# ConvFFN up projection as seven half-width products per tile pair, with the gated activations and the residual spilled to DRAM

## What is computed

```python
def dwconv(x, w, b):            # three taps along the tokens, per channel
    ...
def conv_ffn(hn, w_up, conv_w, conv_b, w_down):
    u = dwconv(hn @ w_up, conv_w, conv_b)
    gate, val = jnp.split(u, 2, axis=-1)
    return (jax.nn.silu(gate) * val) @ w_down
```

## Time and profile before

| | |
|---|---|
| median of three runs | 2789.49 us (2786.89 to 2789.79) |
| the profiled execution, whole | 2791.05 us |
| its span, first to last instruction | 2789.4 us |
| TensorE busy | 97% of the span |
| VectorE, ScalarE, GpSimd busy | 44%, 27%, 7% |
| mean granted TensorE clock | 0.989 |
| DMA | 369 MB, 132 GB/s over the span |

### The profile page before, as it was taken

How to read it: one execution, slowest core, us unless ns; L and a number is a source line. 1 busy time by engine, 2 the same in 40 slices (tenths; PEclk the granted TensorE clock), 3 DMA queues, 4 the chain that set the end, 5 groups by cost and what they waited for, 6 DMA issues and landing times.

```text
span 2789.4 us, 31604 instructions
## 1 busy us (share of the span) xinstructions
PE 2692.7 (97%) x12356; PEld 2087.6 (75%) x12356; DVE 1213.7 (44%) x1282; ACT 746.6 (27%) x840; POOL 194.9 (7%) x197
## 2 busy tenths in 40 slices
PE   4999999999899897999999999999999999999997
PEld 3788888887444444788888888888888888888886
DVE  5534433672543367336533433444334343244345
ACT  3222111222233224223322212232122221132222
POOL 1000000000134145000000000000000000000000
PEclk9999999999999999999999999999999999999999
DMA  9765555783170521422222223222232222322222
GB/s 353 299 236 210 203 204 203 293 307 142 51 151 12 149 77 66 168 90 99 83 95 101 78 93 116 90 90 83 97 106 90 102 84 93 112 90 94 88 93 102
DMA packets 99777, 369.13 MB, mean 132 GB/s; under 512 B 21744, under 2 KB 39200, under 8 KB 69208
## 3 DMA queue, kind: packets, MB, share of 16 engines
q1 hardware_dynamic: 74832, 278.26, 29.3%
q0 software_dynamic: 10880, 72.55, 6.9%
q10 hardware_dynamic: 14000, 17.44, 1.7%
HBM read 346.48 MB, written 21.74 MB: 132 GB/s over the span
## 4 chain that ended last, share of the span: by engine, by line
PE 57%; DVE 1%; DMA 0%; ACT 0%; issue 0%; DVEq 0%; ACTq 0%
PE f_ps L2157 56%; PE f_first_ps L2194 0%; DVE h L2124 0%; PE f_ps L2168 0%; PE f_late_ps L2168 0%; DVE x_lo L2052 0%; DMA h<-in_xT 0%; DVE f_lo L1964 0%; DVE f_square_sum L2004 0%; DMA f_raw<-in_w_out 0%; ACT f_hi L1832 0%; DVE f_full L2046 0%; DVE h L1994 0%; DVE f_square_sum L2000 0%; DVE h L1982 0%
## 5 line engine op out<-in xcount | busy, mean ns | idle before, releaser
L2157 PE MATMUL f_ps<-x_hi,f_hi 128*128 128x512 f32 x1600 | 627.2, 392 | 4.3 <-DVE f_lo L1964 2.5
L2157 PE MATMUL f_ps<-x_hi,f_lo 128*128 128x512 f32 x1600 | 629.6, 393 | 0.0
L2157 PE MATMUL f_ps<-x_lo,f_hi 128*128 128x512 f32 x1600 | 628.2, 393 | 0.0
L1964 DVE TENSOR_TENSOR f_lo<-f_raw,f_hi 128x2048 fp32r<-128x2048 f32 (+1 forms) x164 | 333.3, 2032 | 109.2 <-ACT f_hi L1832 97.0
L1832 ACT ACTIVATE f_hi<-f_raw 128x2048 fp32r<-128x2048 f32 (+1 forms) x164 | 278.6, 1699 | 291.4 <-PE f_ps L2157 285.6
L2157 PEld LDWEIGHTS f_ps<-x_hi,f_hi 128*128 128x128 f32 x1600 | 300.9, 188 | 73.3 <-DVE f_lo L1964 3.3
L2157 PEld LDWEIGHTS f_ps<-x_lo,f_hi 128*128 128x128 f32 x1600 | 300.9, 188 | 69.3
L2157 PEld LDWEIGHTS f_ps<-x_hi,f_lo 128*128 128x128 f32 x1600 | 300.7, 188 | 66.8
L2157 PE MATMUL f_ps<-f_u_hi,f_hi 128*128 128x512 f32 x682 | 267.9, 393 | 0.0
L2157 PE MATMUL f_ps<-f_u_lo,f_hi 128*128 128x512 f32 x682 | 267.4, 392 | 0.0
L2157 PE MATMUL f_ps<-f_u_hi,f_lo 128*128 128x512 f32 x682 | 267.0, 392 | 0.0
(11 more groups left out here) (309 smaller groups left out, 3113.3 us busy)
## 6 DMA issues: line engine op xcount, KB each, us to landing
f_raw<-in_w_up SPq DMA_DIRECT2D x86, 1024.0 KB, 4.8
i_ring<-in_ada_rest POOLq DMA_DIRECT2D x64, 1024.0 KB, 5.3
f_raw<-in_w_down SPq DMA_DIRECT2D x64, 704.0 KB, 4.1
i_raw<-in_w_in SPq DMA_DIRECT2D x38, 1024.0 KB, 4.8
i_ring<-in_ada_first SPq DMA_DIRECT2D x32, 1024.0 KB, 7.4
f_raw<-in_w_out SPq DMA_DIRECT2D x16, 1024.0 KB, 4.8
g_ring<-rrow SPq DMA_DIRECT2D x24, 256.0 KB, 3.6
i_raw<-in_w_first POOLq DMA_DIRECT2D x16, 320.0 KB, 5.1
```

The source lines that it names most:

```text
L1964: nc.vector.tensor_tensor(w_lo[s][:, 0:kt, :], raw[s][:, 0:kt, :], w_hi[s][:, 0:kt, :].bitcast(F32), ALU.subtract).then_inc(lo_ok, 1)
L2157: mm = nc.tensor.matmul(pt[s][:, :], w[s][:, k, :], v[:, c, :], start=(k == 0 and n == 0), stop=(k == len(slots) - 1 and n == 2))
```

## The change

In the up projection, two tile pairs (`PLAIN = 2`) are computed as before. Each of the 42 others (`PAIRS`) is computed as a 2 by 2 block product, with one level of Strassen's scheme in Winograd's form. The blocks of the weights are: gate tile with k steps 0 to 7 (a11) and 8 to 15 (a12), value tile likewise (a21, a22). The blocks of the input are k steps 0 to 7 and 8 to 15, each for the early and the late 256 tokens. Instead of eight block products there are seven (q = 0 to 6), each of 8 k steps and three passes: 24 matmuls of 128x256.

- Weights: GpSimd makes four sums of blocks per pair, each 128x1024 (`block_sums`). ScalarE and VectorE split the seven left operands into high and low parts (`block_high`, `block_low`, 128x1024 each) in four half-tile slots.
- Input: GpSimd makes four sums of input blocks once, in place in the memory of `h`, as 32 operations of 128x256; ScalarE and VectorE split them (`form_high`, `form_low`).
- Outputs: some products accumulate on top of each other in PSUM. ScalarE copies four of the partial results into an SBUF tile `f_c` (`part_copy`), VectorE adds three (`part_add`). The taps then read `f_c` instead of PSUM (`block_middle`, `block_outer`).
- Memory: the gated product's parts are written to DRAM by SyncE (`put_u`, 44 tiles of 512 KB) and read back by GpSimd's queue ahead of each group's down tiles. The residual `h` is written to DRAM tile by tile by GpSimd's queue, since its memory is used for the sums, and read back before the first down tile ends.
- Order: all up tiles come first, then the 64 down tiles, group by group. `normed` writes in place into `h`. The first pair's weights lose their own staging: they go through `raw[0]` and `raw[1]`, whose loads wait until the output projection's last tiles are split.

```diff
-        first_raw = [ground.at("f_first_raw0", [P, KT, P], 0), ground.at("f_first_raw1", [P, KT, P], 106112)]
...
+        bank = [[pt[0], pt[1], pb[0]], [pb[1], pf[0], pf[1]]]
+        SLOT = (0, 1, 2, 3, 0, 1, 2)
+        FIRST_ORDER, ORDER = (0, 1, 2, 3, 4, 5, 6), (3, 0, 1, 2, 4, 5, 6)
...
+            @block.gpsimd
+                for m in range(KT):
+                    pool.wait_ge(ev_ok, m + 1)
+                    pool.dma_start(hd[:, m, :], h[:, m, :]).then_inc(h_st[max(0, m - KT + 3)], 16)
...
+                for k in range(HK):
+                    pool.wait_ge(hl, KT + k + 1)
+                    nc.gpsimd.tensor_tensor(h[:, k, LATE], h[:, k, LATE], h[:, k, EARLY], ALU.subtract).then_inc(ts_ok, 1)
+                for k in range(HK):
+                    pool.wait_ge(hl, KT + HK + k + 1)
+                    pool.wait_ge(ts_ok, HK)
+                    nc.gpsimd.tensor_tensor(h[:, HK + k, LATE], h[:, HK + k, LATE], h[:, k, LATE], ALU.subtract).then_inc(ts_ok, 1)
...
+                def block_sums(i, par, r):
+                    a11, a12, a21, a22 = (block_of(par, n) for n in range(4))
+                    s0, s1, s2 = (b[:, :, :] for b in S_buf)
+                    pool.wait_ge(sl[par], 32 * (r + 1))
+                    if positive(i):
+                        pool.wait_ge(bl_ok, split_by(i - 1, 5))
+                    nc.gpsimd.tensor_tensor(s0, a21, a22, ALU.add).then_inc(bs_ok, 1)
+                    pool.wait_ge(bs_ok, 4 * i + 1)
+                    nc.gpsimd.tensor_tensor(s1, s0, a11, ALU.subtract).then_inc(bs_ok, 1)
+                    nc.gpsimd.tensor_tensor(s2, a11, a21, ALU.subtract).then_inc(bs_ok, 1)
+                    pool.wait_ge(bs_ok, 4 * i + 2)
+                    pool.wait_ge(bl_ok, split_by(i, 1))
+                    nc.gpsimd.tensor_tensor(s0, a12, s1, ALU.subtract).then_inc(bs_ok, 1)
...
+            def block_high(act, i, q, par, r):
+                if q in (0, 3, 6):
+                    act.wait_ge(sl[par], 32 * (r + 1))
+                else:
+                    act.wait_ge(bs_ok, 4 * i + (1, 2, None, 3, 4)[q - 1])
+                if q >= 4:
+                    act.wait_ge(pq_ok, 7 * i + q - 3)
+                elif positive(i):
+                    act.wait_ge(pq_ok, 7 * (i - 1) + (5, 6, 7, 4)[q])
...
+                nc.scalar.activation(slot_of(w_hi, q), source(par, q), ACT.Copy).then_inc(bh_ok, 1)
...
-                    act.wait_ge(first_ld[s], 16)
-                    nc.scalar.activation(first_hi[s][:, :, :], first_raw[s][:, :, :], ACT.Copy).then_inc(hi_ok, 1)
+                    act.wait_ge(w_ld[s], 16 * (KT // 2 + 1))
+                    nc.scalar.activation(first_hi[s][:, :, :], raw[s][:, :, :], ACT.Copy).then_inc(hi_ok, 1)
...
+                    if n == KT + HK:
+                        act.wait_ge(w_ld[1], 16 * (KT // 2 + 2))
+                        nc.scalar.activation(w_hi[1][:, :, :], raw[1][:, :, :], ACT.Copy).then_inc(hi_ok, 1)
...
+            def block_low(dve, i, q, par):
+                dve.wait_ge(bh_ok, split_by(i, q))
+                nc.vector.tensor_tensor(slot_of(w_lo, q), source(par, q), slot_of(w_hi, q).bitcast(F32), ALU.subtract).then_inc(bl_ok, 1)
...
+                def opening(i, par):
+                    block_low(dve, i, 4, par)
+                    u_low(dve, i - 1 + PLAIN, 1 - par)
+                    block_low(dve, i, 5, par)
+                    block_low(dve, i, 6, par)
...
+                def closing(i, par):
+                    last = isinstance(i, int) and i == PAIRS - 1
+                    part_add(dve, i, 3, par)
...
+                        block_low(dve, i + 1, 3, 1 - par)
+                    part_add(dve, i, 4, par)
...
+                        block_low(dve, i + 1, 0, 1 - par)
+                    part_add(dve, i, 5, par)
...
+                        block_low(dve, i + 1, 1, 1 - par)
...
+                    block_outer(dve, i, 0)
+                    block_outer(dve, i, 1)
...
+                        block_low(dve, i + 1, 2, 1 - par)
+                    times(dve, i + PLAIN, (cv_ok, 2 * i + 2))
...
+            def part(pe, i, q, par):
+                pe.wait_ge(bl_ok, split_by(i, q))
...
+                for k in range(HK):
+                    high, low = form(q, k)
+                    for n, (w, v) in enumerate(((a, high), (a, low), (b, high))):
+                        mm = nc.tensor.matmul(to[:, 0:HALF_T], w[:, k, :], v, start=(q in (0, 1, 3) and k == 0 and n == 0),
+                                              stop=(k == HK - 1 and n == 2), skip_group_check=True)
+                mm.then_inc(pq_ok, 1)
```

More of the change, by code:

```diff
@@ L1692, in stage_tail @@
 def stage_tail(nc, A, out, ground, ps, sem, ones, eps, mod, sc_ffn, gfcol, early):
-    UP = 2 * GT
-    PER = UP + KT
-    SLOTS = GT + 1
-    with ExitStack() as ctx:
[L1698 to L1708, removed]
-        x_hi, x_lo, x_raw = early["x_hi"], early["x_lo"], early["x_raw"]
+    PLAIN = 2
@@ new lines, in _ @@
+                for i in range(2):
+                    turn(i, i)
+                with sp.Fori(1, PAIRS // 2 - 1) as r:
+                    for s in range(2):
+                        turn(2 * r + s, s)
+                last = PAIRS - 1
+                sp.wait_ge(bl_ok, split_by(last - 1, 6))
+                for s in range(2):
+                    load_down(0, s, s)
+                put_u(last - 1 + PLAIN, 0)
+                for n in range(3):
+                    sp.wait_ge(h_st[n], 16 if n else 16 * (KT - 2))
@@ new lines, in _, with get_u, kept @@
+                turns(pool, block_sums)
+                def get_u(g, a, b, signal):
+                    for j in range(a, b):
+                        pool.dma_start(u_in[g % 2][j][:, :, :], ud[GT * g + j, :, :, :]).then_inc(signal, 16)
+                def kept(tiles):
+                    for n in range(2):
+                        pool.wait_ge(u_st[n], 32 * ((tiles + 1 - n) // 2))
+                last = PAIRS - 1
+                kept(GT)
+                pool.wait_ge(pq_ok, 7 * last + 2)
@@ L1922, in place @@
[L1922 to L1931 removed]
+                middle(act, 0, 0)
@@ L2093, in ups @@
-                def ups(g):
-                    with dve.Fori(1, GT - 1) as j:
-                        pair(g, j, KT)
-                    pair(g, GT - 1, KT if g + 1 < GROUPS else GT)
-                pair(0, 0, KT)
-                ups(0)
+                split_lo_into(dve, F0 + 4, w_lo[1], raw[1], w_hi[1])
+                times(dve, 0, (ev_ok, F0 + 2))
+                for k in range(HK):
+                    form_low(dve, 1, k)
+                u_low(dve, 0, 0)
+                for k in range(HK):
+                    form_low(dve, 2, k)
@@ L2099, in _, with turn @@
+                def turn(i, par, r):
+                    if not (isinstance(i, int) and i == 0):
+                        opening(i, par)
+                    closing(i, par)
+                turns(dve, turn)
+                split_lo(dve, D0 + 1, 1, GT)
+                u_low(dve, FT - 1, 1)
                 for g in range(GROUPS):
                     final = g == GROUPS - 1
-                    if not final:
-                        pair(g + 1, 0, GT)
-                    t = down_tile(g, 0)
@@ L2228, in _ @@
[L2228 to L2235 removed]
+                    product(pe, F0 + 2 + s, s, every, in_hi, in_lo, free=(read_ok, 1 + s))
```

559 lines of the change are left out of this document (402 added, 157 removed).

## The result

The changed kernel takes 2823.68 us (median of four runs, 2820.87 to 2826.23), beside 2788.19 for the kernel before (four runs, 2785.55 to 2789.79): a ratio of 1.0126, with a 95% interval of 1.0114 to 1.0138. It is slower by 35 us; the forecast was slower by 11. The profiled run took 2826.23 us, 35.2 above the profiled run of before, with a span of 2824.6.

A forecast was written before the change was run, and what follows sets the result against it. TensorE bounds the old kernel; the new bound is mutually exclusive VectorE and GpSimd SBUF work, 22.0 us per pair. Terms sum to +11 on 2791.05: 2802 profiled, 2800 us median; range 2760 to 2840 (80%).

The forecast's parts named there:

- 40 pairs in the middle, -4: Up projection loop: 22.0 us per pair instead of 22.1, -4 us, bounds -56 to +32.
- First and last pair, -4.2: Both ends of the up loop: these two pairs run at TensorE's pace, 2 x -2.1 us.
- First pair's weights, +3.5: Opening: without own staging their second load waits for the output projection's last low part, +3.5 us (2 to 6).
- Input sums +10, ScalarE +1: Late half's normalizing: 32 input-block sums hold VectorE back, +10 us (4 to 15); ScalarE's extra high part, +1 (0 to 2).
- Pair 0 in addition, +3.7: First block pair: leftover VectorE form work and GpSimd's first block sums make product 2 wait, +3.7 us (0 to 8).
- "the loads are a pair ahead. 0.": DMA: spilling 23 MB out and in costs 0, since the DMA is busy a quarter of the time and loads run ahead.
- Hand-over to the down tiles, +1: Up to down tiles: three 512 KB reads issued one product ahead, 8.4 us for 1.5 MB, +1 us (0 to 3).
- Down tiles, 0: Down projection: 33 matmuls per tile, the same work at the same 0.230 us, so no change.
- TensorE stays the bound: Rival for the up loop: the exclusion does not hold or the work fits into gaps; -80 us, 2709 us; 10%.
- Losses covered: Rival for the up loop: exclusion holds but its losses are covered, 21.2 to 21.7 us per pair, 2768 to 2788; 20%.
- GpSimd keeps the turn between its second and third sum: Rival for the up loop: VectorE's low part comes 2.2 us later, 22.6 to 22.9 us per pair, 2824 to 2836; 18%.
- The clock falls: Rival for the up loop: TensorE's clock drops in the new gaps, 2.4 us per pair, about 2895 us; 5%.

The follow-up runs named there:

- the PSUM run: Changed kernel with the assembled conv input in two idle PSUM banks, so the four taps read PSUM again, nothing left out: 2745.21 us, ratio 0.9848 to the kernel before.
- the run without the sums: Changed kernel with the 32 sums of input blocks at the opening cut to 16 of their 256 columns: 2812.43 us (one run).
- small sums: Changed kernel with each of GpSimd's four block sums cut to 16 of 1024 elements from the second block pair on: 2742.38 us (one run).
- fills: Changed kernel with each block sum, from the second block pair on, replaced by a 16-element sum and two fills reading nothing from SBUF: 2740.74 us (one run).

## Why the prediction was right, and where it was wrong

The mechanism in the loop and the sign were right, but the size was not: +35 us for +11, with the missing 24 at the start and the end of the loop. The largest decision, that the exclusion and not TensorE sets the loop's pace, came out to the number: 22.05 us per pair for 22.0. The rows of 4.51 and 1.21 us bore it, and the two operations in 0.89 us bore the exemption that the PSUM run then used.

- *40 pairs in the middle, -4*: -2.2. The 22.0 was a sum of 22.4 with savings and losses of 1.65 and 1.3, and held to 0.05; the savings and losses were not measured one by one, so that some of this closeness may be luck. TensorE's wait came where it was put, ahead of product 2, 1.9 us at most.
- *First and last pair, -4.2*: the last one as said; the first is buried in the step to pair 1.
- *First pair's weights, +3.5*: 3.2.
- *Input sums +10, ScalarE +1*: 9.2 together, and 9.0 by the run without the sums, at the same clock.
- *Pair 0 in addition, +3.7*: 7.5, within its bound of 8. The gap ahead of product 0 (3.4 us) was missing: VectorE still makes low parts of the input forms there, which were priced as one queue ahead of product 2 alone.
- *"the loads are a pair ahead. 0."*: this **step failed**: the step from pair 0 to pair 1 costs 12 us, 6.5 of them one wait behind the load. It is true of the loop and not of pair 1, whose buffer is the memory of `h`. A load can't be ahead of the last reader of what it overwrites, and in the code SyncE's wait on `tl_ok` says which reader that is. The price was there to be worked out: the forms end beside pair 0, and 2 MB take 8.7 us, nearly twice the landing of the earlier trace rows.
- *Hand-over to the down tiles, +1*: this **step failed** as well, 11.2. It priced three reads by their own bytes. They lie behind 3 MB of `h`: without these the last of them lands in 10.9 us instead of 18.3, and the wait of 6.1 is gone. The other wait, 3.2, is for a read issued three products earlier (landed after 12.7 us), which had no term at all; what it waits for is open.
- *Down tiles, 0*: 0.230 us and 465.73 for 2022 matmuls, as said.

Of the 24 us by which the sum was short, the step to pair 1 is 12, the hand-over 10 and pair 0 4, and the rest cancels to -2: the stages ahead -1.6, the opening's terms -2.1, the 40 pairs +1.8.

The rivals: *TensorE stays the bound* is refuted by the waits. *Losses covered* too, the loop is at 22.05. *GpSimd keeps the turn between its second and third sum* gave 2824, and the kernel takes 2824, but for another reason: the low part at 1818.62 goes between the two sums, 22.6 per pair was not reached, and the time comes from start and end. A rival that hits the number isn't thereby the cause. The rule of the Trainium skill (SBUF — State Buffer, on the shared ports) by which that rival was weighed, that whoever issues first holds the ports, agrees with the timelines here, where the low part of 1818.62 goes ahead of the sum of 1819.48, and not with the sum of 990.58 in the earlier trace rows. *The clock falls*: it does, 11 times in the loop, behind waits of 1.7 to 1.8 us, under half of the 4.1 us that the rival had to go by. But it falls in one pair of four and not in each, and where it falls the next wait is missing, so the 2.4 us per pair of that rival don't come. With no waits (the runs with small sums, fills and taps from PSUM) it doesn't fall in the loop. Behind the waits of the start and the hand-over it falls too.

One row was misread without harm: the 0.42 us of an addition from PSUM was taken from an operation on SBUF (L2000 in the earlier trace rows); measured are 0.41.

Not tried: whether the order at the sums would change with VectorE's work moved, and what pair 0's two gaps cost each, since no run took away its form parts alone.

## What to carry to other kernels

When a faster scheme for TensorE moves additions to VectorE and GpSimd, add up both engines' two-operand SBUF work in one column against TensorE's new pace, and not engine by engine: 14.2 and 9.4 us looked harmless under 20, and together they ate the whole gain. An operation next to the limit can be taken out of that column by reading one operand from PSUM: here that was worth 78 us for four taps per pair. And price the first and the last turn of a loop by themselves, from the last reader of the memory that its first load overwrites and from all that is asked of the DMA at the same moment. When two profiled runs are compared, measure from the same event in both: here the stages ahead of the change, alike in all, differ by up to 8.6 us (1273.73 to 1282.30 in the changed kernel and its variants).

## What the runs showed of the hardware

- A GpSimd operation that reads no operand (fills of 1801 and 416 ns, one beside the other for 335 us of 770) doesn't lengthen VectorE's low parts (1.23 us) or taps (0.75), while sums of the same length lengthen a low part to 2.6 us on average.
- The exclusion doesn't care for size: a sum of 16 columns, 0.22 us alone, took 0.66 where it came behind a tap.
- Of two engines that both have work queued, none went twice in a row in the pair shown, while at 990.58 in the earlier trace rows GpSimd's next one went ahead. What decides there is open.
- The hand-over's DMA moves 0.40 to 0.42 MB per us and no more, whether 22 or 11 reads of 512 KB are asked for with the 3 MB read; the landing of the first group's last read, 18.2 or 18.3 us, only fell (to 10.9) with the 3 MB gone.
- TensorE's clock can fall to its lower level behind waits of 1.7 to 1.8 us: behind 11 of the 30 waits in the loop it did, for 15 to 17 matmuls (granted clock 0.50 from 1811 to 1814 us), and behind the others of up to 1.9 us it did not. What decides there isn't shown.
